# Expert loop of a hybrid decoder step: a gather moved behind the first K tile, and the first weight reload cut in three

## What is computed

```python
logits = (xt @ w_router + b_router).astype(jnp.float32)
top_v, top_i = lax.top_k(logits, TOP_K)          # 4 of 32 experts
gates = jax.nn.softmax(top_v, axis=-1)
...
def expert_block(args):
    xb, e = args
    gu = xb @ w_gate_up[e] + b_gate_up[e]        # 1024 -> 2048
    gate, up = gu[:, :D_EXPERT], gu[:, D_EXPERT:]
    gate = jnp.minimum(gate, SWIGLU_LIMIT)
    up = jnp.clip(up, -SWIGLU_LIMIT, SWIGLU_LIMIT)
    act = (up + 1.0) * (gate * jax.nn.sigmoid(SWIGLU_ALPHA * gate))
    return act @ w_down[e] + b_down[e]           # 1024 -> 1024
```

## Time and profile before

| what | us |
|---|---|
| median of 3 runs | 1370.63 |
| lowest and highest | 1369.03, 1375.04 |
| the profiled execution, its own time | 1370.19 |
| its span, first to last instruction | 1368.50 |
| TensorE busy | 1326.8 |

### The profile page before, as it was taken

The page is one execution under the profiler, slowest core; times in us unless marked ns, Lnnn a source line. Parts: engine busy times, 40 slices in busy tenths (PEclk is TensorE's granted clock), DMA queues, the critical chain, the costliest instruction groups (busy, mean ns, idle before and its releaser), DMA issues.

```text
span 1368.5 us, 16670 instructions
## 1 busy us (share of the span) xinstructions
PE 1326.8 (97%) x6823; PEld 733.3 (54%) x6823; DVE 420.9 (31%) x1092; ACT 259.7 (19%) x586; POOL 37.1 (3%) x57
## 2 busy tenths in 40 slices
PE   9999999999999999999999999999999999989997
PEld 7888887888887444443443434434334333433443
DVE  3755467785312312212221122111212112112112
ACT  2113463484202110110110101101011010101102
POOL 0000012110000000000000000000000000000000
PEclk9999999999999999999999999999999999999999
DMA  9444457898997899999999999999999999999994
GB/s 251 154 140 142 153 172 246 281 343 268 266 310 327 326 415 408 433 431 433 428 429 431 434 428 430 433 428 433 431 429 431 429 433 431 431 431 429 429 425 187
DMA packets 93876, 488.93 MB, mean 357 GB/s; under 512 B 8505, under 2 KB 73529, under 8 KB 78297
## 3 DMA queue, kind: packets, MB, share of 16 engines
q1 hardware_dynamic: 84384, 460.46, 83.2%
q0 software_dynamic: 4608, 24.41, 5.2%
q10 hardware_dynamic: 4809, 2.98, 0.8%
HBM read 476.91 MB, written 11.19 MB: 357 GB/s over the span
## 4 chain that ended last, share of the span: by engine, by line
PE 74%; DMA 23%; SPq 1%; ACT 1%; DVE 1%; issue 0%; ACTq 0%; POOL 0%; POOLq 0%; DVEq 0%
PE bank L314 72%; DMA ring<-in_w_gate_up 12%; DMA ring<-in_w_down 3%; DMA plain_conv<-in_w_gate_up 3%; DMA plain_conv<-in_w_down 3%; PE bank L938 2%; DMA ring<-in_w_proj_b 1%; SPq L371 1%; DMA ring<-ac_dram 1%; ACTq L665 0%; ACTq L663 0%; POOLq L65 0%; DVE ring L1643 0%; ACT L858 0%; DVE ring L1673 0%
## 5 line engine op out<-in xcount | busy, mean ns | idle before, releaser
L314 PE MATMUL bank<-ring,plain_conv 128*64 128x512 f32 (+1 forms) x1312 | 299.5, 597 | 9.9 <-DMA ring<-in_w_gate_up 9.9
L314 PE MATMUL bank<-exn,ring 128*128 128x264 f32 (+1 forms) x1168 | 263.8, 389 | 0.2 <-DVE exn L1468 0.2
L314 PEld LDWEIGHTS bank<-exn,ring 128*128 128x128 f32 (+1 forms) x1168 | 218.6, 190 | 40.8 <-issue 3.2
L314 PEld LDWEIGHTS bank<-ring,plain_conv 128*64 128x64 f32 (+1 forms) x1312 | 93.0, 138 | 189.6 <-issue 171.8
L314 PE MATMUL bank<-plain_conv 128*64 128x512 f32 (+2 forms) x848 | 183.6, 582 | 8.3 <-DMA plain_conv<-in_w_gate_up 7.9
L314 PE MATMUL bank<-ring,exn 128*64 128x512 f32 x576 | 127.6, 595 | 3.2 <-DMA ring<-in_w_down 3.2
L314 PEld LDWEIGHTS bank<-plain_conv 128*64 128x64 f32 (+2 forms) x848 | 58.9, 138 | 122.9 <-issue 108.5
L1859 DVE TENSOR_TENSOR xT<-xT,bank 128x264 f32<-128x264 f32 x128 | 55.0, 429 | 222.7 <-PE bank L314 220.9
L1865 DVE TENSOR_SCALAR bank<-bank 128x512 f32<-128x512 f32 x31 | 21.7, 700 | 316.4 <-PE bank L314 316.4
L314 PE MATMUL bank<-plain_conv,exn 128*64 128x512 f32 (+1 forms) x422 | 99.9, 590 | 1.9 <-DMA plain_conv<-in_w_down 1.6
L847 ACT ACTIVATE exn<-bank 128x512 f32<-128x512 f32 x31 | 18.5, 598 | 412.6 <-DVE bank L1865 412.6
(11 more groups left out here) (294 smaller groups left out, 850.3 us busy)
## 6 DMA issues: line engine op xcount, KB each, us to landing
ring<-in_w_gate_up SPq DMA_DIRECT2D x35, 4096.0 KB, 38.3
plain_conv<-in_w_gate_up SPq DMA_DIRECT2D x23, 4096.0 KB, 40.0
ring<-in_w_down SPq DMA_DIRECT2D x16, 4096.0 KB, 39.8
plain_conv<-in_w_down SPq DMA_DIRECT2D x11, 4096.0 KB, 37.8
ring<-in_w_in SPq DMA_DIRECT2D x36, 1024.0 KB, 5.4
ring<-in_w_gate_up SPq DMA_DIRECT2D x8, 2048.0 KB, 10.6
ring<-in_w_down SPq DMA_DIRECT2D x5, 2048.0 KB, 8.7
ring<-in_w_proj_b SPq DMA_DIRECT2D x8, 1024.0 KB, 10.5
```

Source lines behind the costliest of these rows:

```text
L314: return nc.tensor.matmul(out, w, x, start=start, stop=stop)
```

## The change

Two things are moved in the first pair of each pass, and one transfer is cut.

1. `gather_second` stands no longer ahead of `value_load` and the loop (and no longer in the block for later passes), but inside `pair`, behind `gate_up(0, 0)`.
2. The first reload (unit 5 into buffer 0) comes in pieces of 1 MB (rows 0 and 1 of 8), 1 MB (rows 2 and 3) and 2 MB (rows 4 to 7). The first waits for a new semaphore `half_used`, raised at the end of `gate_up(0, 0)`; the second for the `w_used` that the first half waited for before; the third for the same as the second half before.
3. The second piece lands on `columns_landed[0]`, and TensorE waits for it ahead of row 2 of `down(1)` of the first pair. `half_used` also takes the place of `second_used` at the end of the pass.

```diff
             def load_pairs(p):
 
-                load_pair(p, 0, 0, first=5, split=(5,))
+                sp.wait_ge(S["half_used"], 2 * p + 1)
+                load_rows(0, 5, 0, 0, 2, unit_landed[0])
+                sp.wait_ge(S["w_used"], 2 * UNITS * PAIRS * p + 1)
+                load_rows(0, 5, 0, 2, 4, columns_landed[0])
+                sp.wait_ge(S["w_used"], 2 * UNITS * PAIRS * p + 2)
+                load_rows(0, 5, 0, 4, 8, half_landed[0])
                 load_pair(p, 0, 1, split=range(5))
...
             ins.then_inc(S["early_filled"], 1)
-            gather_second()
             pe.wait_ge(S["passes_ready"], 1)
             n_passes = pe.value_load(passes[TS - 1:TS, 0:1], min_val=1, max_val=MAXP)
...
+                    if first and x == k == 0:
+                        ins.then_inc(S["half_used"], 1)
                     if k % 2:
                         ins.then_inc(S["w_used"], 1)
...
                     for s in rows:
+                        if first and x and s == 2:
+                            pe.wait_ge(columns_landed[0], 48 * p + 16)
                         if s == 4:
                             second_half(4 + x)
...
-                        pe.wait_ge(columns_landed[half], 32 * p + 32)
+                        pe.wait_ge(columns_landed[half], (48 - 16 * half) * (p + 1))
                         return unit[(q + 4 + x) % PLACES]
...
                     gate_up(0, k)
+                    if first and k == 0:
+                        gather_second()
                     if first and k == 1:
                         gather(p_first[1], RIGHT).then_inc(S["xt_filled"], 1)
...
                     gather(p_early, range(2)).then_inc(S["early_filled"], 1)
-                    gather_second()
                 pair(p, 0, 0, first=True)
```

More of the change, by code:

```diff
@@ L278, in build @@
             pick_e_ready pick_ready rms_ready router_loaded sg_ready silu_done smp_ready sqrt_done
-            sq0_ready ssq0_set st_done u_ready u_filled u_taken usq_ready part_ready urms_ready rstd_ready second_used ug_ready vec_loaded vec_set w_used wdec_exp wdec_in logits_filled rank0_filled rank12_filled early_filled early_taken
+            sq0_ready ssq0_set st_done u_ready u_filled u_taken usq_ready part_ready urms_ready rstd_ready half_used ug_ready vec_loaded vec_set w_used wdec_exp wdec_in logits_filled rank0_filled rank12_filled early_filled early_taken
             pick0_ready last_left parts_filled parts_taken
@@ L376, in load_half, with load_rows @@
                              unit_of(j, c)[:, rows * h:rows * h + rows, :].rearrange("p s n -> p (s n)")).then_inc(landed, 16)
+            def load_rows(j, c, n, r0, r1, landed):
+                sp.dma_start(unit[n][:, D * r0:D * r1], unit_of(j, c)[:, r0:r1, :].rearrange("p s n -> p (s n)")).then_inc(landed, 16)
             def load_columns(j, c, n, h, landed):
@@ L456, in _ @@
                     load_pairs(p)
-            sp.wait_ge(S["second_used"], n_passes)
+            sp.wait_ge(S["half_used"], 2 * n_passes)
             sp.dma_start(n_final, a["norm_final"].rearrange("(o d) -> o d", o=1).to_broadcast([P, D])).then_inc(S["final_loaded"], 16)
@@ L1367, in pair @@
                 if final:
-                    ins.then_inc(S["second_used"], 1)
+                    ins.then_inc(S["half_used"], 1)
                 for k in range(KT):
```

## The result

| | before | changed |
|---|---|---|
| median, us | 1370.32 (20 runs) | 1374.38 (20 runs) |
| lowest and highest | 1368.85, 1375.04 | 1371.96, 1377.05 |
| the profiled execution, span | 1368.5 | 1374.2 |

The ratio is 1.0028, with a 95% interval from 1.0022 to 1.0034: 3.8 us slower (3.0 to 4.7). That is within 0.5% and in the range, but more than the 1.6 of the forecast (1372.2); it is nearly the 1373.9 of the rival "the clock falls as well".

What follows compares the result with a forecast made beforehand. The prediction took the time to follow buffer releases at 513 and 524 us, set by TensorE. The profiled 1370.19 plus 1.6 for the gather, other terms 0, gave 1371.8; with 0.44 for the runs' median, 1372.2 us, range 1370.2 to 1376.5.

Steps and rivals of the forecast that it cites:

- the clock falls as well: Rival: after the new idle time TensorE's clock falls, 1.69 more on top of 1.6, so 1373.9 us; chance 0.34.
- What bounds the kernel: Up to 524 us: the time follows the buffer releases at 513 and 524 us, and these follow TensorE.
- The first K tile doesn't start earlier: At 446.0 us: the sequencer's chain holds `gate_up(0, 0)` even without the gather; gain 0 to 0.2 us, taken as 0.
- The gather's price: Between K tiles 0 and 1: the 12 moved matmuls are laid open, 1.53 to 1.65 us, taken as 1.6.
- The clock: TensorE idle from 444.37 to 446.02: half clock might cost 1.69 us; left out of the forecast, kept in the range.
- No wait swallows it: Behind the moved gather: no later wait, the 0.80 us one for the gates included, absorbs the delay; swallowed 0.
- The transfers: First reload: first piece issued 1.8 us earlier; bounds a gain of 1.8 and a loss of 0.5, taken as 0.
- the early start counts: Rival: with the stream the bound from 446 us on, the first megabyte 1.8 earlier gives 1368.8 us; chance 0.07.
- Out of instructions: Rival: at the entry of the loop over passes TensorE lacks instructions, 6.0 us in all, 1376.6 and up; chance 0.09.
- What a measurement can tell: For the whole kernel: 6.9 us, 0.5%, is about the least a measurement can tell from no change.
- the likeliest case: The forecast itself: the gather's 1.6 us alone, clock not falling, 1372.2 us; chance 0.42.

Runs made afterwards that it cites:

- e5: The kernel before with 12 matmuls, result overwritten, ahead of the second pair, so ahead of the releases at 513 and 524 us: ratio 1.0024.
- e6: The kernel before with 12 matmuls, result overwritten, ahead of the fourth pair, behind the release at 524 us: ratio 1.0007.
- e7: The kernel before with the four reloads behind the first six cut in halves too: ratio 0.9996.
- e4: The changed kernel with TensorE running one pass as a constant, without load, loop or branch for the number of passes: ratio 1.0008.
- e3: The changed kernel with 6 matmuls, result overwritten, in the idle time that the moved gather left: ratio 1.0008.
- e2: The kernel before with only the gather moved, the first reload still in two halves: ratio 1.0026.
- e1: The changed kernel with the gather in its old place, so only the first reload's split: median 1369.81 us, ratio 0.9990.
- e8: The kernel with only the first reload's split, gather in its old place, measured a second time: ratio 1.0001.
- e9: The changed kernel run once more for its profile: 928.3 us from the early gather's start to the end.
- e10: The changed kernel run a third time for its profile: 930.6 us from the early gather's start to the end.

## Why the prediction was right and where it was off

- **What bounds the kernel: right.** e5 and e6 show it directly; e7 shows that the 358 GB/s at 515 to 527 were a standstill for want of released buffers.
- **The first K tile doesn't start earlier: right.** Gain taken 0, bounds 0 to 0.2; the profiles of the changed kernel have 2.88, 3.03 and 3.02 against 3.00. e4 shows that the sequencer's chain holds it.
- **The gather's price: right in kind, small in size.** Term 1.6, bounds 1.53 and 1.65; e3 measures 1.87. The bounds were rows of gathers alone; what they lacked is that gathers between weight matmuls of two K tiles part those too (0.15), and the 12 matmuls took 1.72, not 1.65. The 1.72 stood in the earlier trace rows: 20 matmuls in 3.07 with the gather, 8 in 1.35 without.
- **The clock: the step that failed.** The prediction left the term out ("the rows leave it a little under even"), with 0.34 for it; it fell in five of five profiles with new idle time. The step took six idle times of like length in the loop as six draws for this one, and minded length only, though the idle time here stands behind other work. The loop was no guide to this place: over all profiles it would have said one in six. The size was a little short as well: 1.69 as in one row, but 1.4 to 2.7 measured, on the mean 2.0, because half clock can last for nearly all of 447 to 454, and matmuls of the gather lie in it. What the Trainium skill's "Perfetto Trace Analysis", section Matmul Optimizations, says, that matmuls should run back to back because power follows utilization, agrees with the five falls; it was the better guide.
- **No wait swallows it: right.** The 0.80 wait for the gates is in the changed kernel too, and R follows K tile 2 to 0.01 in every kernel with the gather moved (4.55 and 4.54 in the changed one, 3.32 and 3.32 in e2).
- **The transfers: right at 0**, by e1 and e8. The issue times were off with the clock: 6.59 instead of 4.9 behind the early gather, so in the changed kernel the first megabyte leaves only 0.11 earlier than the first two did. The rival "the early start counts" (1368.8) is dead by R in e1; the runs of e1 alone wouldn't have said so.
- **Out of instructions: not as put.** There is no such standstill at the entry of the loop over passes (the branch took 0.25), but there is another one further on; see the last section.
- **What a measurement can tell: too coarse.** The 6.9 us were called about the least that can be told from no change; 20 runs of each kernel told 3.8, with an interval of 3.0 to 4.7.

Forecast 1372.2, measured 1374.4. The range held because it took in the rival with the clock, and not because the likeliest case came true, which was the wrong one of two: with the clock's 2.0 and the gather's 1.87 the sum would have read 1374.5.

## What to carry to other kernels

In this kernel, ahead of the last standstill of the stream, only TensorE's own work counted: look for its idle time, not for bytes that could go sooner. Before moving work away from the front of a wait, read what else fills that time, the sequencer's loads and branches included: the gather that ran under them was free, and in its new place it cost 1.87. And an idle time that a reorder opens on TensorE can cost more than its length, as clock behind it: here it did so in five profiles of five, in the loop one time in six, so the rows of another place don't give the chance. The cheapest test is to fill it with matmuls that nobody reads.

## What the runs showed of the hardware that was not expected

**Half clock after an idle time of 0.72 us** (e4, one profile), and after 1.5 to 1.7 in four of four, where in the loops of all profiles idle times of that length brought it 12 times in 72. It ended with K tile 0 (e9) or lasted into the gather behind it (the four others).

**The same fall at the last wait for weights** (e8 against e1, 1.7 us) adds to the spread of the runs: what comes after it has no wait left that could take it.

**A second standstill for "issue".** In the loop, at the jump back, before has one of 2.92. All profiles of kernels with the gather moved and the loop over passes kept (changed, e2, e3, e9, e10) have another of 3.6 to 4.3 a few matmuls on; the others have none. In the changed kernel:

```profile
1013.95 1.09 PE L314 MATMUL bank<-exn,plain_conv 32*64 32x512 f32 x8 [2.33 <-issue]
1014.96 0.64 PE L314 MATMUL bank<-ring,plain_conv 128*64 128x512 f32 x1
1019.79 8.78 PE L314 MATMUL bank<-ring,plain_conv 128*64 128x512 f32 x31 [4.18 <-issue]
```

Nothing was edited at that place; what these kernels share is that their code stands otherwise, which may be the reason. It costs nothing here that shows (e3 has it, and ends 1.8 later with a release 1.96 later), since TensorE waits for weights again behind it; in a kernel bound by TensorE there it would be 4 us. Its cause wasn't tried and stays open.
